# Pre-norm squares in column groups, a second block started inside the first, first weights in quarters: a two-block fp32 model on one core

## The chip, the core and the metric
The kernel runs on one core of one Trainium2 chip. The metric is device time in microseconds (us) of one execution; lower is better. Of the core's engines four compute: TensorE (PE, matmuls into PSUM), VectorE (DVE), ScalarE (ACT) and GpSimd (POOL). SyncE (SP) issues most DMAs. Every engine runs its own instructions in order, and they wait for each other by semaphores.

## What is computed
A residual stream h of 272 tokens (16 meta tokens and 256 of the input) by 1024 features goes through two blocks of a first model and one of a second. The parts, in the order of their weights' names:

```
for i in 0, 1:                       # the first model
    f = swiglu(rms_norm(h, g), w_gu, w_down);  h = h + 0.5 * rms_norm(f, g')     # gu0/dn0, gu2/dn2
    m = short_conv_mixer(...) if i == 0 else diff_attention_mixer(...)           # conv_in/out, qkv/attn_out
    h = h + rms_norm(m, g'')
    f = swiglu(rms_norm(h, ...), ...);         h = h + 0.5 * rms_norm(f, ...)    # gu1/dn1, gu3/dn3
h = h[:, 16:]                        # the second model
h = h + mixers(rmsnorm(h)) @ w_out                                               # mix_in, mix_out
h = h + square(relu(rmsnorm(h) @ w_ff1)) @ w_ff2                                 # ff1, ff2
out = rmsnorm(h)
```

All is float32. rms_norm(t, g) is t * rsqrt(mean(t * t) + eps) * g over the features. Nine of these norms are "pre-norms", of h itself: eight ahead of a matrix product and the final one.

## The kernel before
h lies with features on partitions, as eight tiles of 128 x 272 (k = 0 to 7). The weights, 225 MB, are streamed once as blocks of 16, 22 or 24 tiles of 128 x 128 into four buffers w_raw. To keep float32 accuracy at the speed of the fp32r type, each operand is split in a high part (rounded to fp32r) and a low part (the rest): w = w_hi + w_lo, x = x_hi + x_lo. A product is then three fp32r passes per tile, w_hi x_hi, w_hi x_lo and w_lo x_hi (lines 1370 to 1372). ACT makes w_hi (`split_hi`, line 446) and DVE makes w_lo (`split_lo`, line 813). There are two buffers of each, so the split of block n waits until TensorE has used block n - 2. Inside each engine's program the split of block i + 2 (`next_hi`, `next_lo`) is written between the elementwise work on block i; that place in the program sets when it can start.

A pre-norm is not applied to the input. x is h times the gain; the product is made with it, and the result is multiplied by rstd, which is known later. So at the entry of every part, `first_block` (line 1387) goes through k: two or three x_hi matmuls with w_hi and with w_lo, then those with x_lo, and then `add_square` (line 1381), a plain f32 matmul of `ones` with the square of h tile k, which adds up the sum over features in PSUM bank `SUM`. ACT makes x_hi and the square for each k (`pre_norm`), and its square k waits for the squares matmul of k - 2. After the eighth, `root` makes rstd: DVE takes ms from PSUM, ACT does Ln and Exp (lines 470, 472), DVE three Newton steps (829 to 834). DVE then multiplies the block's results by rstd (`take`, line 868), ACT applies silu, and so on.

Ahead of six of the eight entries stands a post-norm (`post_norm`, line 849): h is updated tile by tile by DVE (scaled, h, x_lo), while TensorE runs `keep_warm`, seven f32 matmuls of 384 columns on constants (line 1436). At the start, SP loads the first weight block whole, then the parameters, then h, then three more blocks.

The second block's split of each entry is made between the post-norm's root and the pre-norm (`second_hi`) and after the x_lo parts (`second_lo`).

## Times and profile before
| | us |
|---|---|
| median of 3 runs | 1453.66 |
| lowest, highest | 1453.46, 1454.67 |
| the profiled execution's own time | 1454.77 |
| its span, first to last instruction | 1453.0 |
| TensorE busy | 1402.9 (97%) |
| VectorE, ScalarE busy | 896.7 (62%), 653.5 (45%) |
| mean granted TensorE clock | 0.992 |

In the rows below, PE is TensorE's matmuls and PEld its weight loads. A row of a timeline gives the start, the time, the engine, the line of the kernel, the operation, out<-in, and in brackets how long the engine was idle before it and what ended that. An f32 matmul shows as two records (x2). The time of a matmul's record includes its way through the array; where matmuls follow each other, the distance of their starts is what one costs.

### The profile page before, as it was taken

The page shows a single profiled execution, that of the slowest core. Times are in us where ns is not written, and L with a number is a line of the kernel's source. Part 1 is how long each engine was busy: PE and PEld are TensorE (multiplying, and loading weights), DVE is VectorE, ACT ScalarE, POOL GpSimd, SP SyncE. Part 2 cuts the span into 40 slices and gives each one's busy share as a digit, 9 for nine tenths or more (in the row PEclk, how much of TensorE's full clock was granted, in tenths as well). Part 3 has the DMA queues.
Part 4 walks back from the last instruction along what each step waited for, and adds up shares of the span by engine and source line. Part 5 has one row for each costly group of instructions (what it writes and reads, how often), then busy time and mean ns, then how long its engine had stood idle before and what let it go on. Part 6 is the DMA issues. An engine that isn't in the chain of part 4 may idle for free.

```text
span 1453.0 us, 26632 instructions
## 1 busy us (share of the span) xinstructions
PE 1402.9 (97%) x10924; PEld 1361.8 (94%) x10924; DVE 896.7 (62%) x1329; ACT 653.5 (45%) x925; POOL 12.5 (1%) x26
## 2 busy tenths in 40 slices
PE   6999999999999999999999999999999997999997
PEld 6999999998999999999998988999998986899997
DVE  4666547657666537666457877666546566577543
ACT  5444435345444435444444555544535425444332
POOL 0000000000000000000000000000001100000000
PEclk9999999999999999999999999999999999999999
DMA  6555543343555433555553223455653411355550
GB/s 241 174 173 206 199 173 131 131 135 126 173 174 205 174 142 117 173 173 210 181 183 112 82 84 117 167 181 192 231 184 127 175 59 59 125 194 180 196 175 30
DMA packets 29353, 227.54 MB, mean 157 GB/s; under 512 B 3376, under 2 KB 4672, under 8 KB 5088
## 3 DMA queue, kind: packets, MB, share of 16 engines
q1 hardware_dynamic: 28656, 224.75, 44.0%
q0 software_dynamic: 624, 1.77, 0.3%
q8 instruction: 51, 0.84, 0.2%
q14 instruction: 22, 0.18, 0.0%
HBM read 225.44 MB, written 1.06 MB: 156 GB/s over the span
## 4 chain that ended last, share of the span: by engine, by line
PE 84%; DVE 10%; ACT 4%; issue 2%; DMA 0%; DVEq 0%; ACTq 0%
PE ps L1370 24%; PE ps L1372 24%; PE ps L1371 24%; DVE w_lo L813 4%; PE ps L1384 2%; ACT w_hi L446 2%; PE ps L1436 2%; PE ps L1395 1%; PE ps L1396 1%; PE ps L1400 1%; ACT s_exp L594 1%; DVE small L1009 0%; PE ps L1576 0%; PE ps L1578 0%; PE ps L1577 0%
## 5 line engine op out<-in xcount | busy, mean ns | idle before, releaser
L813 DVE TENSOR_TENSOR w_lo<-w_raw,w_hi 128x2048 fp32r<-128x2048 f32 (+2 forms) x188 | 482.0, 2564 | 232.7 <-ACT w_hi L446 232.7
L1370 PE MATMUL ps<-x_hi,w_hi 128*128 128x272 f32 (+1 forms) x2136 | 616.1, 288 | 5.9 <-DVE w_lo L813 5.7
L1372 PE MATMUL ps<-x_hi,w_lo 128*128 128x272 f32 (+1 forms) x2136 | 612.5, 287 | 0.0
L1371 PE MATMUL ps<-x_lo,w_hi 128*128 128x272 f32 (+1 forms) x2136 | 610.7, 286 | 0.0
L446 ACT ACTIVATE w_hi<-w_raw 128x2048 fp32r<-128x2048 f32 (+2 forms) x188 | 401.1, 2134 | 425.9 <-PE ps L1372 420.1
L1370 PEld LDWEIGHTS ps<-x_hi,w_hi 128*128 128x128 f32 x2136 | 403.8, 189 | 13.4 <-DVE w_lo L813 7.2
L1372 PEld LDWEIGHTS ps<-x_hi,w_lo 128*128 128x128 f32 x2136 | 403.9, 189 | 0.0
L1371 PEld LDWEIGHTS ps<-x_lo,w_hi 128*128 128x128 f32 x2136 | 403.5, 189 | 0.3 <-issue 0.2
L1370 PE MATMUL ps<-hid_hi,w_hi 128*128 128x272 f32 (+1 forms) x960 | 276.1, 288 | 0.2 <-DVE w_lo L813 0.2
L1372 PE MATMUL ps<-hid_hi,w_lo 128*128 128x272 f32 (+1 forms) x960 | 274.8, 286 | 0.0
L1371 PE MATMUL ps<-hid_lo,w_hi 128*128 128x272 f32 (+1 forms) x960 | 273.7, 285 | 0.0
L1370 PEld LDWEIGHTS ps<-hid_hi,w_hi 128*128 128x128 f32 x960 | 181.0, 189 | 0.8 <-issue 0.4
L1371 PEld LDWEIGHTS ps<-hid_lo,w_hi 128*128 128x128 f32 x960 | 181.0, 189 | 0.2
L1372 PEld LDWEIGHTS ps<-hid_hi,w_lo 128*128 128x128 f32 x960 | 181.0, 189 | 0.0
L872 DVE TENSOR_TENSOR gate<-rstd,ps 128x272 f32<-128x272 f32 (+1 forms) x88 | 38.2, 434 | 106.8 <-PE ps L1372 106.2
L504 ACT ACTIVATE square<-ps 128x272 f32<-128x272 f32 (+1 forms) x40 | 15.8, 395 | 152.7 <-PE ps L1372 150.7
L1395 PE MATMUL ps<-x_hi,w_hi 128*128 128x272 f32 (+1 forms) x152 | 54.1, 378 | 12.8 <-DVE w_lo L813 10.0
L905 DVE TENSOR_TENSOR sumsq<-sumsq,square 128x272 f32<-128x272 f32 (+1 forms) x42 | 18.3, 435 | 65.0 <-ACT square L504 64.8
L480 ACT ACTIVATE square<-h 128x272 f32<-128x272 f32 (+1 forms) x72 | 30.2, 420 | 34.7 <-PE ps L1384 24.0
L1384 PE MATMUL ps<-square,ones 128*128 128x272 f32 (+1 forms) x144 | 45.0, 395 | 0.6 <-ACT square L480 0.6
L1395 PEld LDWEIGHTS ps<-x_hi,w_hi 128*128 128x128 f32 x152 | 29.6, 195 | 16.3 <-issue 13.5
L842 DVE SCALAR_TENSOR_TENSOR x_lo<-h,par,x_hi 128x272 fp32r<-128x272 f32 (+1 forms) x64 | 31.3, 492 | 21.5 <-ACT x_hi L493 21.5
...
## 6 DMA issues: line engine op xcount, KB each, us to landing
w_raw<-w_gu SPq DMA_DIRECT2D x88, 1024.0 KB, 4.9
...
w_raw<-w_ff SPq DMA_DIRECT2D x32, 1024.0 KB, 4.9
...
w_raw<-w_conv_out SPq DMA_DIRECT2D x4, 1024.0 KB, 4.8
w_raw<-w_attn_out SPq DMA_DIRECT2D x4, 1024.0 KB, 5.0
```

The costliest lines, as they stand in the source:

```text
L446: act.activation(w_hi[j % SPLIT][:, 0:width], w_raw[j][:, 0:width], ACT.Copy).then_inc(hi_ready, 1)
L480: act.activation(square[k % 2][:, c0:T], h[:, k, c0:T], ACT.Square).then_inc(h_sq_ready, 1)
L813: dve.tensor_tensor(w_lo[j % SPLIT][:, 0:width], w_raw[j][:, 0:width], w_hi[j % SPLIT][:, 0:width].bitcast(F32), ALU.subtract).then_inc(lo ...
L842: dve.scalar_tensor_tensor(out=x_lo[:, k, c0:T], in0=h[:, k, c0:T], scalar=par[:, g:g + 1], in1=x_hi[:, k, c0:T].bitcast(F32), op0=ALU.mul ...
L872: dve.tensor_tensor(gate[j % 2][:, 0:width], rstd[:, c0:T], ps[:, 2 * (j % 2), c0:T], ALU.mult)\
L905: dve.tensor_tensor(sumsq[:, c0:T], sumsq[:, c0:T], square[par_][:, c0:T], ALU.add).then_inc(sumsq_ready, 1)
L1370: pe.matmul(out_ap, w_hi[slot][:, cols], hi(k), start=first, stop=False)
L1371: pe.matmul(out_ap, w_hi[slot][:, cols], lo(k), start=False, stop=False)
L1372: mm = pe.matmul(out_ap, w_lo[slot][:, cols], hi(k), start=False, stop=last)
L1384: pe.matmul(ps[:, SUM, c0:T], ones[:, :], square[k % 2][:, c0:T], start=k == 0, stop=k == KD - 1)\
L1395: pe.matmul(o, w_hi[0][:, cols], x_hi[:, k, c:T], start=k == 0, stop=False)
L1436: pe.matmul(ps[:, 5, 0:3 * P], ones[:, :], sq3[:, :], start=True, stop=True)
```

## The change
Nothing that is computed changes but the way in which the squares are added. The parts:
- **Squares in groups.** The squares of all eight tiles go to fx (free at that time) and no longer to two small buffers, so ACT doesn't wait for TensorE between them. `group_squares` multiplies them with 32 columns of ones each, tile k into the column group k mod 4 of the array, accumulated in PSUM; ACT copies the result, scaled by 1/32, to SBUF (`copy_groups`), and `sum_groups` adds the groups with one matmul of ones. Both stand later than the squares did: after the low passes of the second block and at its end in an ffn and ff1; between the three products of the second block in conv_in and mix_in; after the first block and in the second in qkv.
- **Ahead.** In gu1, gu2, gu3 and ff1, `first_block` also makes, for each k, the passes w_hi x_hi of the second block (two) and one of the two w_hi x_lo; `second_block` does the rest. The first block's results lie in banks 4 and 5.
- **Splits earlier.** ACT's split of the third block stands ahead of the root (ffn, conv_in, ff1), DVE's too in an ffn and in ff1, but not in conv_in.
- **post_norm** on DVE: h of tile k directly after scaled of tile k (x_lo of k - 2 between them).
- **First weights in pieces.** The first block comes in four DMAs, each a quarter of the columns of both halves (rows of 1 KB), h in four DMAs and the parameters, issued by ACT; the first splits go by quarters.
- **Warming** with 26 fp32r passes of 272 (256) columns.
- The mixers' low part has a tile of its own, and its g_q memset waits for that matmul.

```diff
-            def add_square(q, k, c0):
-                pe.wait_ge(h_sq_ready, KD * q + k + 1)
-                pe.matmul(ps[:, SUM, c0:T], ones[:, :], square[k % 2][:, c0:T], start=k == 0, stop=k == KD - 1)\
-                  .then_inc(h_sq_summed, 1)
+            def group_squares(q, c0, count=KD):
+                for k in range(count):
+                    g = GROUP * (k % GROUPS)
+                    pe.wait_ge(h_sq_ready, KD * q + k + 1)
+                    mm = pe.matmul(ps[g:g + GROUP, SUM + 1, c0:T], ones[:, 0:GROUP], fx[:, k, c0:T],
+                                   start=k < GROUPS, stop=k + GROUPS >= count, tile_position=(0, g))
+                mm.then_inc(h_sq_grouped, 1)
+            def sum_groups(q, c0):
+                pe.wait_ge(h_sq_copied, q + 1)
+                pe.matmul(ps[:, SUM, c0:T], ones[:, :], h_sum[:, c0:T], start=True, stop=q < 8).then_inc(h_sq_summed, 1)
...
-                    add_square(q, k, c0)
+                    for s, (o, c) in enumerate(ahead):
+                        cols = slice((s * KD + k) * P, (s * KD + k + 1) * P)
+                        pe.matmul(o, w_hi[1][:, cols], x_hi[:, k, c:T], start=k == 0, stop=False)
+                        if s == 0:
+                            pe.matmul(o, w_hi[1][:, cols], x_lo[:, k, c:T], start=False, stop=False)
+            def second_block(q, n0, outs, c0, ahead):
+                pe.wait_ge(hi_ready, n0 + 2)
...
+                        if not ahead or s == 1:
+                            pe.matmul(o, w_hi[1][:, cols], x_lo[:, k, c0:T], start=False, stop=False)
+                group_squares(q, c0)
+                split_ready(n0, 1)
...
+                        mm = pe.matmul(o, w_lo[1][:, cols], x_hi[:, k, c0:T], start=False, stop=k == KD - 1)
+                mm.then_inc(block_used, 1)
+                sum_groups(q, c0)
...
-                pe.wait_ge(consts_loaded, 16)
-                for _ in range(count):
-                    pe.matmul(ps[:, 5, 0:3 * P], ones[:, :], sq3[:, :], start=True, stop=True)
+                warm = y_hi[:, 0, :] if u == 1 else z_hi[:, 0, :] if u == 4 else hid_hi[:, first_col(u):T]
+                for _ in range(26):
+                    pe.matmul(ps[:, 5, 0:warm.shape[-1]], warm[:, 0:P], warm, start=True, stop=True)
...
                     for s in range(3):
                         mm = product(ps[:, b + s, 0:T], j % 2, s * KD, KD, hi, lo)
+                        if isinstance(i, int) and i == 1 and s < 2:
+                            (group_squares if s == 0 else sum_groups)(q, 0)
...
# ACT, pre_norm
-                if KD * q + k >= 2:
-                    act.wait_ge(h_sq_summed, KD * q + k - 1)
-                act.activation(square[k % 2][:, c0:T], h[:, k, c0:T], ACT.Square).then_inc(h_sq_ready, 1)
+                act.activation(fx[:, k, c0:T], h[:, k, c0:T], ACT.Square).then_inc(h_sq_ready, 1)
...
+                if name:
+                    next_hi(name, count, 0, 0)
+                copy_groups(q, c0)
                 root(s, c0)
...
+            act.dma_start(par[:, :], params).then_inc(par_loaded, 16)
+            for q in range(PIECES):
+                ks = slice(q * KD // PIECES, (q + 1) * KD // PIECES)
+                act.dma_start(h[:, ks, :], h_in[:, ks, :]).then_inc(h_landed[q], 16)
# DVE, root
+                if meanwhile:
+                    next_lo(*meanwhile, 0, 0)
                 dve.wait_ge(summed, count)
...
-                pre_root(u, s, c0)
+                pre_root(u, s, c0, *((f"gu{f}", GU_N) if kind == "ffn" else ()))
```

What stands in a row on the engines, at two places. First TensorE at the entry of gu1, from the last warming to the end of the first k step (w_hi, w_lo are the parts of the weights, the first block's except in lines 1473 and 1475, which are the second's), before:

```order
L1436 MATMUL ps<-sq,ones 128x384 x7
L1395 MATMUL ps<-x_hi,w_hi 128x272
L1396 MATMUL ps<-x_hi,w_lo 128x272
L1395 MATMUL ps<-x_hi,w_hi 128x272
L1396 MATMUL ps<-x_hi,w_lo 128x272
L1400 MATMUL ps<-x_lo,w_hi 128x272 x2
L1384 MATMUL ps<-square,ones 128x272
```

And after, with the end of the loop and the rest of the second block:

```order
L1463 MATMUL ps<-x_hi,w_hi 128x272
L1464 MATMUL ps<-x_hi,w_lo 128x272
L1468 MATMUL ps<-x_lo,w_hi 128x272 x2
L1473 MATMUL ps<-x_hi,w_hi 128x272
L1475 MATMUL ps<-x_lo,w_hi 128x272
L1473 MATMUL ps<-x_hi,w_hi 128x272
L1486 MATMUL ps<-x_lo,w_hi 128x272 x8
L1438 MATMUL ps<-fx,ones 32x272 x8
L1492 MATMUL ps<-x_hi,w_lo 128x272 x16
L1445 MATMUL ps<-h_sum,ones 128x272
```

The square left the step, three passes of the second block came in, and the eight squares and their sum stand in the second block. Second, VectorE at the entry of conv_in, from the split of the second block (line 813, later 853) to that of the third, before:

```order
L813 TENSOR_TENSOR w_lo<-w_raw,w_hi 128x3072
L827 TENSOR_SCALAR ms<-ps 128x272
L829 TENSOR_TENSOR rstd<-r 128x272
L831 SCALAR_TENSOR_TENSOR rstd<-rstd,ms 128x272
L834 SCALAR_TENSOR_TENSOR rstd<-rstd,r 128x272
L923 TENSOR_TENSOR rstd_sq<-rstd 128x272
L924 MEMSET cv_u 128x2
L932 TENSOR_TENSOR cv_c<-rstd_sq,ps 128x272
L933 TENSOR_TENSOR cv_b<-rstd,ps 128x272
L935 TENSOR_TENSOR cv_u<-cv_c,ps 128x272
L813 TENSOR_TENSOR w_lo<-w_raw,w_hi 128x3072
```

And after:

```order
L853 TENSOR_TENSOR w_lo<-w_raw,w_hi 128x3072
L875 TENSOR_SCALAR ms<-ps 128x272
L877 TENSOR_TENSOR rstd<-r 128x272
L879 SCALAR_TENSOR_TENSOR rstd<-rstd,ms 128x272
L882 SCALAR_TENSOR_TENSOR rstd<-rstd,r 128x272
L971 TENSOR_TENSOR rstd_sq<-rstd 128x272
L972 MEMSET cv_u 128x2
L980 TENSOR_TENSOR cv_c<-rstd_sq,ps 128x272
L981 TENSOR_TENSOR cv_b<-rstd,ps 128x272
L983 TENSOR_TENSOR cv_u<-cv_c,ps 128x272
L853 TENSOR_TENSOR w_lo<-w_raw,w_hi 128x3072
```

Here nothing moved on VectorE; what ms waits for did, on TensorE.

## Rows read from the trace of the kernel before

**Rows 1.** The page: busy time and share by engine; shares of the chain.
```profile
PE 1402.9 (97%) x10924; PEld 1361.8 (94%) x10924; DVE 896.7 (62%) x1329; ACT 653.5 (45%) x925; POOL 12.5 (1%) x26
...
PE 84%; DVE 10%; ACT 4%; issue 2%; DMA 0%; DVEq 0%; ACTq 0%
```

**Rows 2.** Chain of waits, entry of gu1: start, us, what.
```profile
333.06 4.52 PE ps L1436 x14
...
338.32 0.46 PE ps L1384 x2
```

**Rows 3.** Waits of PE: us in total, times, longest.
```profile
PE ps L1395 <- DVE w_lo L813: 10.0, 1, 10.0
PE ps L1370 <- DVE w_lo L813: 7.9, 9, 2.2
...
PE ps L1395 <- ACT x_hi L493: 2.8, 2, 2.5
```

**Rows 4.** Timeline of PE, gu1: start, us, work [idle before].
```profile
337.11 0.58 PE L1395 MATMUL ps<-x_hi,w_hi 128*128 128x272 f32 x1
...
354.37 0.39 PE L1370 MATMUL ps<-x_hi,w_hi 128*128 128x272 f32 x1 [0.69 <-DVE w_lo L813]
...
360.51 0.29 PE L1370 MATMUL ps<-x_hi,w_hi 128*128 128x272 f32 x1
```

**Rows 5.** Timeline of ACT and DVE, entry of gu1.
```profile
336.22 0.52 ACT L493 ACTIVATE x_hi<-h,par 128x272 fp32r<-128x272 f32 x1 [0.84 <-DVE h L860]
...
347.29 0.44 DVE L827 TENSOR_SCALAR ms<-ps 128x272 f32<-128x272 f32 x1
...
350.12 0.44 DVE L872 TENSOR_TENSOR gate<-rstd,ps 128x272 f32<-128x272 f32 x1
...
351.80 0.41 ACT L514 ACTIVATE gate<-gate 128x272 f32<-128x272 f32 x1
...
351.93 2.29 DVE L813 TENSOR_TENSOR w_lo<-w_raw,w_hi 128x2048 fp32r<-128x2048 f32 x1 [1.01 <-ACT w_hi L446]
```

**Rows 6.** Timeline of DVE, entry of conv_in.
```profile
234.90 3.35 DVE L813 TENSOR_TENSOR w_lo<-w_raw,w_hi 128x3072 fp32r<-128x3072 f32 x1
238.32 0.44 DVE L827 TENSOR_SCALAR ms<-ps 128x272 f32<-128x272 f32 x1
...
242.68 3.35 DVE L813 TENSOR_TENSOR w_lo<-w_raw,w_hi 128x3072 fp32r<-128x3072 f32 x1
```

**Rows 7.** Timeline of ACT and PE at the start.
```profile
5.62 1.91 ACT L446 ACTIVATE w_hi<-w_raw 128x2048 fp32r<-128x2048 f32 x1 [3.53 <-DMA w_raw<-w_gu]
...
9.96 0.56 PE L1395 MATMUL ps<-x_hi,w_hi 128*128 128x272 f32 x1 [9.96 <-DVE w_lo L813]
...
23.70 0.59 PE L1370 MATMUL ps<-x_hi,w_hi 128*128 128x272 f32 x1 [2.23 <-DVE w_lo L813]
```

**Rows 8.** Groups by line and form: count, busy us, mean ns, idle before.
```profile
L1283 DVE TENSOR_TENSOR hid<-hid 128x512 f32<-128x512 f32 x16 | 11.1, 692 | 0.5
...
L763 ACT ACTIVATE hid_hi<-hid 128x512 f32 x12 | 7.4, 616 | 2.1 <-DVE hid L1283 2.1
```

**Rows 9.** Timeline of PE, one scores step of the attention.
```profile
792.05 0.97 PE L1533 MATMUL ps<-k_rot,q_rot 64*128 64x144 f32 x8 [0.32 <-DVE k_rot L1001]
792.96 0.40 PE L1370 MATMUL ps<-x_hi,w_hi 128*128 128x272 f32 x1
```

**Rows 10.** Windows: us, busy by engine (x), PEclk (granted), DMA share, GB/s.
```profile
24.00:27.00 3.00, 3.00 (x14) 3.00 (x14) 1.95 (x5) 2.91 (x4) 0.00 (x0) 0.50 0.65 202
...
306.90:310.30 3.40, 1.47 (x12) 1.25 (x12) 2.58 (x2) 1.56 (x3) 0.00 (x0) 1.00 0.02 5
310.40:313.70 3.30, 3.30 (x17) 3.30 (x16) 1.64 (x3) 2.51 (x3) 0.00 (x0) 0.50 0.76 233
```

**Rows 11.** DMA issues: KB each, median us from issue to landing.
```profile
w_raw<-w_gu SPq DMA_DIRECT2D x88, 1024.0 KB, 4.9
...
h<-h_in SPq DMA_DIRECT2D x1, 1088.0 KB, 6.7
```

More of the change, by code:

```diff
@@ L62 @@
 RAW, SPLIT = 4, 2
+PIECES = 4
+GROUPS = 4
+GROUP = P // GROUPS
 SLOT = TRI_T * P
@@ L549, in step @@
                 def step(i, j, last=False):
-                    if not last:
+                    if not last and i > 0:
                         next_hi("conv_in", TRI_N, i, j)
@@ L760, in step @@
                 def step(i, j):
-                    next_hi("ff1", FF1_N, i, j)
+                    if not isinstance(i, int) or i > 0:
+                        next_hi("ff1", FF1_N, i, j)
                     act.wait_ge(hid_ready, i + (4 * KF + 1))
@@ L764, in step @@
                        .then_inc(hid_hi_ready, 1)
-                loop(act, FF1_N, step, peel=2)
+                step(0, 0)
+                loop(act, FF1_N, step, first=1, peel=2)
+            act.dma_start(par[:, :], params).then_inc(par_loaded, 16)
+            for q in range(PIECES):
+                ks = slice(q * KD // PIECES, (q + 1) * KD // PIECES)
+                act.dma_start(h[:, ks, :], h_in[:, ks, :]).then_inc(h_landed[q], 16)
             act.preload_act_table_set(LN_EXP_SET)
-            split_hi(0, 0, WIDTH[0])
             act.wait_ge(eps_ready, 2)
@@ L775, in _ @@
                 c0 = first_col(u)
-                pre_norm(u, s, c0, pre)
+                pre_norm(u, s, c0, pre, *{"ffn": (f"gu{f}", GU_N), "conv": ("conv_in", TRI_N), "attn": ()}[kind])
                 s += 1
@@ L1288, in step @@
                        .then_inc(hid_lo_ready, 1)
-                loop(dve, FF1_N, step, peel=2)
+                step(0, 0)
+                loop(dve, FF1_N, step, first=1, peel=2)
             def second_lo(q):
@@ L1402, in first_block @@
                         mm.then_inc(block_used, 1)
-                    add_square(q, k, c0)
+                    for s, (o, c) in enumerate(ahead):
[4 more added lines that the diff above has]
+            def second_block(q, n0, outs, c0, ahead):
+                pe.wait_ge(hi_ready, n0 + 2)
+                for s, o in enumerate(outs):
+                    for k in range(KD):
+                        cols = slice((s * KD + k) * P, (s * KD + k + 1) * P)
+                        if not ahead:
+                            pe.matmul(o, w_hi[1][:, cols], x_hi[:, k, c0:T], start=k == 0, stop=False)
+                        if not ahead or s == 1:
+                            pe.matmul(o, w_hi[1][:, cols], x_lo[:, k, c0:T], start=False, stop=False)
+                group_squares(q, c0)
+                split_ready(n0, 1)
+                for s, o in enumerate(outs):
+                    for k in range(KD):
+                        cols = slice((s * KD + k) * P, (s * KD + k + 1) * P)
+                        mm = pe.matmul(o, w_lo[1][:, cols], x_hi[:, k, c0:T], start=False, stop=k == KD - 1)
+                mm.then_inc(block_used, 1)
+                sum_groups(q, c0)
             def hidden(name, f, q, c0):
@@ L1452, in convolution @@
                 hi, lo = x_parts(0)
-                first_block(q, n0, [(ps[:, s, 0:T], 0) for s in range(3)], 0)
+                first_block(q, n0, [(ps[:, s, 0:T], 0) for s in range(3)])
                 def step(i, j):
@@ L1629, in mixers @@
                     if i == 0:
-                        first_block(q, n0, [(ps[:, s, 0:SEQ], META) for s in range(3)], META)
-                        pe.wait_ge(mix_loaded, 6 * 16)
-                        pe.wait_ge(mix_zeroed, 4)
-                        pe.matmul(ps[0:HEADS, 7, :], rel_sb[:, :], onehot_sb[:, :], start=True, stop=True)\
-                          .then_inc(dist_done, 1)
+                        first_block(q, n0, [(ps[:, s, 0:SEQ], META) for s in range(3)])
                         continue
@@ L1641, in mixers @@
                         mm = product(ps[:, 3 * (i % 2) + s, 0:SEQ], i % 2, s * KD, KD, hi, lo)
+                        if i == 1 and s < 2:
+                            (group_squares if s == 0 else sum_groups)(q, META)
                     mm.then_inc(block_used, 1)
                     if i == 1:
+                        pe.wait_ge(mix_loaded, 6 * 16)
+                        pe.wait_ge(mix_zeroed, 4)
+                        pe.matmul(ps[0:HEADS, 7, :], rel_sb[:, :], onehot_sb[:, :], start=True, stop=True)\
+                          .then_inc(dist_done, 1)
                         pe.wait_ge(low_ready, KD)
@@ L1647, in mixers @@
                         for k in range(KD):
-                            mm = pe.matmul(ps[0:16, 6, 0:SEQ], w_glow_sb[:, k, :], fx[:, k, META:T], start=k == 0, stop=k == KD - 1)
+                            mm = pe.matmul(ps[0:16, 6, 0:SEQ], w_glow_sb[:, k, :], low[:, k, :], start=k == 0, stop=k == KD - 1)
                         mm.then_inc(g_pe, 1)
@@ L1773, in wide_hidden @@
                 hi, lo = x_parts(META)
[L1775 removed]
+                ahead = ((ps[:, 2, 0:SEQ], META), (ps[:, 3, 0:SEQ], META))
+                first_block(q, n0, [(ps[:, AHEAD + s, 0:SEQ], META) for s in range(2)], ahead)
+                second_block(q, n0, [ps[:, 2, 0:SEQ], ps[:, 3, 0:SEQ]], META, ahead)
                 def step(i, j):
                     split_ready(n0, i)
[L1779 removed]
+                    if not isinstance(i, int) or i >= 3:
                         pe.wait_ge(relu_ready, i * 2 - 2)
```

132 lines of the change are left out of this document (87 added, 45 removed).

## The prediction
> **What bounds the kernel now.** I read the page's busy shares and its chain first: TensorE is busy for 97% of the span and holds 84% of the chain that ended last [rows 1]. An edit pays only by taking work off TensorE or by closing one of its waits. The waits are few: 10.0 us ahead of the first matmul, nine waits for a w_lo split that come to 7.9 us (the longest 2.2), and 2.5 us for x_hi ahead of ff1 [rows 3]. Then I read the places where a pre-norm stands, since the change touches little else. There a plain f32 squares matmul stands in the chain with 0.46 us, and seven warming matmuls with 4.52 us [rows 2]; an fp32r pass is far cheaper: 48 of them lie between 354.37 and 360.51, 0.126 us each and 6.05 us a block [rows 4].
>
> **Squares.** Eight at 0.455 us are 3.64 us at each of nine pre-norms. After the change the eight load 32 columns of weights each, for four column groups of the array, and one more f32 matmul (0.455) sums the groups. No row shows column groups. The nearest is the scores stage, where f32 matmuls of 64 rows alternate between the two halves of the array: two products of 144 and two of 272 columns would take 1.39 us one after another, and start at 792.05 with the next matmul at 792.96 [rows 9]: 0.91 us, half of 1.39 and 0.2 for filling and draining. So the halves run side by side. Bounds for the eight are 0.91 us (four side by side) and 3.64 us (none); I take the lower, by that row, and add the 0.2. With the sum it is 1.57 us: TensorE's work falls by 2.1 us a place, 1.95 with 256 columns.
> The Trainium skill, TensorEngine Tiling (Array Packing), Key Properties, says that a change of tiling mode drains the engine: the 0.2 agrees. Its page TensorE: Matmul & The Clock Gate, Measured speedup vs the span model, gives three column groups 2.38 times the speed, not 3; by that the eight would cost an estimated 0.24 us more, 2 us in all; no run here shows it.
>
> **Warming.** 26 fp32r passes take 3.3 us where 4.5 stood: -1.2 us at six places (-1.4 with 256 columns). What they don't cover comes back as a wait for x_hi, counted below.
>
> **What is late next: the root.** The squares' sum stood at the end of the first block; now it stands behind the second block (ffn, ff1) or behind two thirds of it (conv_in, mix_in). rstd moves with it, and behind rstd are queued, on ScalarE and VectorE, the splits of a later block. In an ffn the chain is 2.83 us from ms to gate (347.29 to 350.12), gate 0.44, silu 0.41 [rows 5], w_hi 1.92, w_lo 2.29, hand-overs 0.2: 8.1 us. TensorE has one block to hide it, 6.05 us: it waits 2.05 us ahead of the fourth block, where it had waited 0.69 ahead of the third [rows 4]. In conv_in VectorE's next w_lo starts 4.36 us after ms (238.32 to 242.68) and lasts 3.35 [rows 6]: 8.0 us behind the sum with hand-overs, against one product of 24 passes, 3.0 us: 4.9 us of wait that is not there now. ScalarE's w_hi comes early, but VectorE keeps w_lo behind the root.
>
> **Place by place** (warming, squares, waits after, waits before; minus is a gain).
> - gu1 and gu2: warming ends at 333.06 + 3.3 = 336.4; x_hi, now at 336.22 [rows 5], comes 0.24 earlier (h right behind its scaled), done at 336.5, TensorE starts 0.5 before 337.11. So -1.2 - 2.1 + (0.35 for x_hi + 0.5 for the first x_lo + 2.05) - (0.2 + 0.69) = -1.3 each. The second block's 24 high passes in the loop are moved, not removed: nine passes a k, 1.13 us, about VectorE's pace of three instructions (0.36 to 0.41 each beside one another). Its w_lo is ready before TensorE has done the squares, since the next w_lo stands behind it and ahead of the root: no wait there.
> - gu3: -1.4 - 1.95 + (1.5 + 0.5 + 2.2) - 1.7 = -0.8.
> - conv_in: the first block without squares ends at 224.5 + 0.5 + 72 x 0.126 = 234.1. VectorE, no longer held by the squares, starts w_lo at 232.7 instead of 234.90 [rows 6]; it is ready at 236.1, 2.0 later than TensorE. -1.2 - 2.1 + (0.4 + 2.0 + 4.9) - 0 = +4.0.
> - qkv: -3.3 + (0.6 for x_hi, 1.2 for w_lo, 2.1 for the query's copy, which ScalarE does behind the root, 2.9 for rotary) - 2.1 = +1.4.
> - mix_in: -3.35 + (0.7 + 2.05 + 0.5 + 2.6) = +2.5. The 2.6: eight copies into low, w_hi and a w_lo of 3.35 follow the later root. qkv and mix_in have more links than I can price: 2 us either way each.
> - ff1: -1.95; root 2.8, two relu, square 0.69, hid_hi 0.61 [rows 8], hid_lo 0.69, relu and square again, w_lo 2.29: 9.4 against 5.7, 3.65 waited where 1.0 was: +0.7.
> - Final norm: eight squares off the last products, a group of seven and two f32 matmuls on: -1.6.
> - gu0: TensorE starts at 9.96 behind w_hi (from 5.62) and w_lo, and waits till 23.70 for block two [rows 7]. With quarters ScalarE issues five DMAs (0.42 each, as SP's), loads its table (1.28), is free at 4.2, and does a quarter of w_hi, two x_hi, two squares in 2.05 us: four in 12.4, w_hi of block two at 14.3. TensorE then has 32 passes, squares, 16 passes, sum: 21.9; block three to 28.0, a wait of 2.1: block four starts at 30.1. Now it starts at 37.5 (23.70 + two blocks + 1.5 for the clock below + 0.2): -7.5. The bound on the other side: h took 6.7 us to land, a weight block 4.9 [rows 11], and now rows of 1 KB and two queues share the engines; if the last quarter lands 5 us late, -2.5. I take -7.5.
> Sum: -7.5 + 4.0 - 2.6 - 0.8 + 1.4 + 2.5 + 0.7 - 1.6 = -3.9 us.
>
> **The clock.** After the wait that ends at 23.70 the granted clock is 0.50, the lower level, from 24 to 27; a stretch with 1.47 us busy of 3.40 (1.93 idle) at 307 to 310 is followed by 0.50 too [rows 10]. No wait of 1.5 us in the list [rows 3] was followed by it. At 1.2 GHz a pass takes 0.226 us, so 3.4 us there lose 3.4 x (1 - 0.126 / 0.226) = 1.5. The change has eleven waits of 1.9 to 4.9 us that were shorter or absent. Bounds: none to ten stretches more, 0 to 15 us. Most waits are just above 1.93, so I take four: +6.0.
> Total +2.1. On the profiled execution's own 1454.77 (span 1453.0) it is 1456.9; the median of the runs stands 1.1 below that execution: 1456.
>
> **Rivals.**
> - *The other side, slower: column groups don't overlap.* Place: the eight squares matmuls at nine pre-norms. One at a time they take 3.64 instead of 0.91, 2.7 x 9 = +24.6: 1480. Two at a time +8: 1464. For it: no column group in the trace, and each carries a wait of its own. Against: the halves in the scores stage [rows 9]. From some 2 us for the eight the kernel is slower by more than 0.2%.
> - *Faster: the clock holds.* Seven of the eleven waits are 2.0 to 2.2 us. If none lowers the clock, the sum is -3.9: 1450.
> - *The quarters land late*, so the start is not what the change means it to be: +5: 1461.
>
> **Chances.** Forecast 0.5 (its own range 1450 to 1461, none to seven stretches); no overlap 0.1; two at a time 0.1; clock holds 0.2; late quarters 0.1. 0.2%, 2.9 us, is about what a measurement of this kernel can tell from no change: 1450.8 to 1456.6. Faster takes the clock's case and 0.05 of the forecast's: 0.25. Same takes 0.34 of the forecast's and its neighbours'. Slower the rest, 0.41. Range 1448 to 1472: out are the full loss of overlap and a gain beyond the clock's case.
>
> **What would show it.** The records of the eight squares within 1.3 us; the first matmul near 5.7 us; waits for w_lo of 2 us ahead of the fourth block of each ffn, 4.9 in conv_in, 3.6 in ff1; clock 0.50 behind about half of them. I am wrong if the eight take 2 us or more, if those waits are under 1 us, or if the first matmul starts after 8 us.

## The result, and the profile after

| | before | after |
|---|---|---|
| median of 17 runs, us | 1454.53 | 1462.63 |
| lowest, highest | 1452.64, 1457.69 | 1457.79, 1467.47 |
| mean granted clock over runs (before: 23 later runs) | 0.993 | 0.986 |
| profiled execution's span, us | 1453.0 | 1457.6 |

The ratio is 1.005, 95% interval 1.004 to 1.0061: slower, by 8.1 us of the medians. The forecast was 1456, inside a range that holds 1462.6, and slower was its likeliest sign (0.41); but the forecast's own range ended at 1461, and the median lies where it had put its rivals. The profiled execution (1459.38) is one of the faster ones; the two slowest, 1465.64 and 1467.47, have a granted clock of 0.984 and 0.983, the two fastest 0.989.

Busy time and the chain's shares, on the page of the changed kernel, beside [rows 1]:

```profile
PE 1385.4 (95%) x11014; PEld 1353.4 (93%) x11014; DVE 896.6 (62%) x1332; ACT 655.6 (45%) x937; POOL 12.6 (1%) x26
...
PE 79%; DVE 14%; ACT 5%; issue 2%; DMA 0%; DVEq 0%; ACTq 0%; SPq 0%
```

TensorE's work fell by 17.5 us, and the span rose by 4.6: the chain's share of TensorE went from 84 to 79%, that of VectorE from 10 to 14. The waits of TensorE say where (in all, times, longest), beside [rows 3]:

```profile
PE ps L1422 <- DVE w_lo L853: 25.9, 12, 4.8
PE ps L1463 <- DVE w_lo L867: 6.9, 1, 6.9
PE ps L1463 <- ACT x_hi L524: 6.4, 7, 2.6
PE ps L1629 <- DVE k_rot L1049: 5.7, 8, 1.5
...
PE ps L1422 <- ACT q_sb L605: 1.7, 1, 1.7
```

The one wait at the start fell from 10.0 to 6.9; the waits for w_lo inside rose from 7.9 to 25.9 us. The entry of gu1 on TensorE, beside [rows 4] (x16 are the eight squares, two records each):

```profile
336.80 0.36 PE L1463 MATMUL ps<-x_hi,w_hi 128*128 128x272 f32 x1 [0.36 <-ACT x_hi L524]
...
341.00 0.29 PE L1463 MATMUL ps<-x_hi,w_hi 128*128 128x272 f32 x1
...
347.45 1.12 PE L1438 MATMUL ps<-fx,ones 128*32 128x272 f32 x16
...
348.51 2.27 PE L1492 MATMUL ps<-x_hi,w_lo 128*128 128x272 f32 x16
...
359.29 0.38 PE L1422 MATMUL ps<-x_hi,w_hi 128*128 128x272 f32 x1 [2.01 <-DVE w_lo L853]
```

The eight squares take 1.05 us to the next matmul (1.00 with 256 columns); the loop goes by 1.13 us a k; the third block is reached without a wait, and the fourth waits 2.01. What it waits for, on VectorE, ScalarE and VectorE, beside [rows 5]:

```profile
351.27 0.44 DVE L875 TENSOR_SCALAR ms<-ps 128x272 f32<-128x272 f32 x1 [0.77 <-PE ps L1445]
...
354.10 0.44 DVE L921 TENSOR_TENSOR gate<-rstd,ps 128x272 f32<-128x272 f32 x1
...
354.91 1.90 ACT L466 ACTIVATE w_hi<-w_raw 128x2048 fp32r<-128x2048 f32 x1
...
356.85 2.29 DVE L853 TENSOR_TENSOR w_lo<-w_raw,w_hi 128x2048 fp32r<-128x2048 f32 x1 [0.91 <-ACT w_hi L466]
```

From ms at 351.27 to the end of w_lo at 359.14 it is 7.87 us, and TensorE has one block of 6.05. The entry of conv_in, beside [rows 6]:

```profile
230.15 0.39 PE L1422 MATMUL ps<-x_hi,w_hi 128*128 128x272 f32 x1 [1.76 <-DVE w_lo L853]
...
238.21 0.44 DVE L875 TENSOR_SCALAR ms<-ps 128x272 f32<-128x272 f32 x1 [8.12 <-PE ps L1445]
...
242.57 3.35 DVE L853 TENSOR_TENSOR w_lo<-w_raw,w_hi 128x3072 fp32r<-128x3072 f32 x1
...
245.98 0.55 PE L1422 MATMUL ps<-x_hi,w_hi 128*128 128x272 f32 x1 [4.79 <-DVE w_lo L853]
```

w_lo of the third block (242.57) again stands 4.36 us behind ms, and 4.79 are waited for it. The start, beside [rows 7]:

```profile
5.34 0.63 ACT L471 ACTIVATE w_hi<-w_raw 128x512 fp32r<-128x512 f32 x1 [0.49 <-DMA w_raw<-w_gu]
...
6.87 0.57 PE L1463 MATMUL ps<-x_hi,w_hi 128*128 128x272 f32 x1 [6.87 <-DVE w_lo L867]
...
15.45 0.39 PE L1484 MATMUL ps<-x_hi,w_hi 128*128 128x272 f32 x1 [0.68 <-ACT w_hi L466]
...
31.50 0.39 PE L1422 MATMUL ps<-x_hi,w_hi 128*128 128x272 f32 x1 [2.00 <-DVE w_lo L853]
```

The clock. Stretches of the changed kernel with the columns of [rows 10]; the second and third hold gu1's wait of 2.01, with no fall behind it:

```profile
246.30:249.30 3.00, 3.00 (x15) 3.00 (x15) 2.43 (x7) 1.92 (x2) 0.00 (x0) 0.50 0.72 218
354.90:359.30 4.40, 2.39 (x20) 2.17 (x19) 3.49 (x5) 4.39 (x5) 0.00 (x0) 1.00 0.02 9
359.40:362.40 3.00, 3.00 (x24) 3.00 (x25) 2.96 (x5) 0.86 (x2) 0.00 (x0) 1.00 0.63 205
570.60:573.60 3.00, 3.00 (x15) 3.00 (x15) 2.52 (x2) 0.43 (x1) 0.00 (x0) 0.50 0.80 320
775.30:778.30 3.00, 3.00 (x16) 3.00 (x16) 2.93 (x14) 2.47 (x1) 0.00 (x0) 0.50 0.01 3
904.80:907.80 3.00, 3.00 (x16) 3.00 (x16) 3.00 (x10) 2.25 (x6) 0.00 (x0) 0.51 0.00 0
1280.50:1283.50 3.00, 3.00 (x16) 3.00 (x15) 3.00 (x3) 0.64 (x1) 0.00 (x0) 0.50 0.80 317
```

Five stretches of 3.4 us at 0.50, 1.2 GHz, are new: behind the waits of 4.79 in conv_in, 2.01 in gu2 (569), 1.68 in qkv, two of 1.47 at gu3's entry, and 3.67 in ff1. The one of before at 24 is gone (granted 1.00 there). Both kernels also have one of 3.4 at 310 (after: 311), one of 6.8 at 1205 (1209), one of 3.4 at 1252 (1256) and the last 6.0 (6.7) us of the span, behind TensorE's last matmul.

| part | forecast, without new stretches | measured | of it new stretches |
|---|---|---|---|
| gu0 | -7.5 | -5.8 | 0 |
| conv_in | +4.0 | +5.9 | +1.5 |
| gu1 | -1.3 | -1.3 | 0 |
| gu2 | -1.3 | +0.3 | +1.5 |
| qkv | +1.4 | +1.6 | +1.5 |
| gu3 | -0.8 | +0.5 | +1.5 |
| mix_in | +2.5 | +2.7 | 0 |
| ff1 and the end | -0.9 | +0.8 | +1.5 |
| sum | -3.9 | +4.7 | +7.5 |

Measured is how the difference of the two profiled executions grows from one post-norm's sum of squares to the next (219.07 against 213.29, 330.95 against 331.08, and so on; ff1 by its first matmul and the last one of the program). Without the new stretches it is -2.8, beside the forecast's -3.9; both count the stretch at 24 that went, -1.5.

### The profile page after: what moved, and what is told of

It reads as the page before. It is cut to its first block, busy times and chain, and to the rows that moved or that the text cites. A ratio compares the mean times of both kernels' runs of the same rounds, so it can differ in the third digit from the quotient of the medians.

```text
span 1457.6 us, 26741 instructions
## 1 busy us (share of the span) xinstructions
PE 1385.4 (95%) x11014; PEld 1353.4 (93%) x11014; DVE 896.6 (62%) x1332; ACT 655.6 (45%) x937; POOL 12.6 (1%) x26
## 4 chain that ended last, share of the span: by engine, by line
PE 79%; DVE 14%; ACT 5%; issue 2%; DMA 0%; DVEq 0%; ACTq 0%; SPq 0%
PE ps L1422 24%; PE ps L1424 23%; PE ps L1423 23%; DVE w_lo L853 4%; ACT w_hi L466 2%; DVE scaled L904 1%; DVE h L910 1%; PE ps L1492 1%; DVE x_lo L890 1%; ACT s_exp L627 1%; PE ps L1468 1%; PE ps L1473 1%; PE ps L1438 1%; PE ps L1463 1%; PE ps L1464 1%
## 5 line engine op out<-in xcount | busy, mean ns | idle before, releaser
L1422 PE MATMUL ps<-x_hi,w_hi 128*128 128x272 f32 (+1 forms) x2056 | 595.7, 290 | 25.4 <-DVE w_lo L853 23.7
L1424 PE MATMUL ps<-x_hi,w_lo 128*128 128x272 f32 (+1 forms) x2056 | 590.7, 287 | 0.0
L1423 PE MATMUL ps<-x_lo,w_hi 128*128 128x272 f32 (+1 forms) x2056 | 589.6, 287 | 0.0
L1422 PEld LDWEIGHTS ps<-x_hi,w_hi 128*128 128x128 f32 x2056 | 390.4, 190 | 32.1 <-DVE w_lo L853 17.2
L1424 PEld LDWEIGHTS ps<-x_hi,w_lo 128*128 128x128 f32 x2056 | 390.7, 190 | 0.0
L1423 PEld LDWEIGHTS ps<-x_lo,w_hi 128*128 128x128 f32 x2056 | 389.9, 190 | 0.6 <-issue 0.2
L953 DVE TENSOR_TENSOR sumsq<-sumsq,square 128x272 f32<-128x272 f32 (+1 forms) x42 | 18.3, 435 | 65.0 <-ACT square L538 64.8
L1463 PE MATMUL ps<-x_hi,w_hi 128*128 128x272 f32 (+1 forms) x152 | 42.2, 300 | 13.2 <-DVE w_lo L867 6.9
L1463 PEld LDWEIGHTS ps<-x_hi,w_hi 128*128 128x128 f32 x152 | 30.3, 199 | 14.5 <-issue 14.5
L552 ACT ACTIVATE hid_hi<-up 128x272 f32 (+3 forms) x88 | 36.6, 416 | 14.3 <-DVE up L930 14.3
L1464 PE MATMUL ps<-x_hi,w_lo 128*128 128x272 f32 (+1 forms) x152 | 41.6, 295 | 0.0
L935 DVE TENSOR_TENSOR hid_lo<-up,hid_hi 128x272 f32 (+3 forms) x88 | 37.9, 431 | 2.0 <-ACT hid_hi L552 2.0
```

The lines of the kernel that those rows point to most:

```text
L552: act.activation(hid_hi[:, bass.ds(i * T + c0, width)], up[j % 2][:, 0:width], ACT.Copy)\
L935: dve.tensor_tensor(hid_lo[:, bass.ds(at, width)], up[j % 2][:, 0:width], hid_hi[:, bass.ds(at, width)].bitcast(F32), ALU.subtract).then_i ...
L953: dve.tensor_tensor(sumsq[:, c0:T], sumsq[:, c0:T], square[par_][:, c0:T], ALU.add).then_inc(sumsq_ready, 1)
L1422: pe.matmul(out_ap, w_hi[slot][:, cols], hi(k), start=first, stop=False)
L1423: pe.matmul(out_ap, w_hi[slot][:, cols], lo(k), start=False, stop=False)
L1424: mm = pe.matmul(out_ap, w_lo[slot][:, cols], hi(k), start=False, stop=last)
```

## The experiments

A term of all that follows: with a mean granted clock c and a span S, 2 x (1 - c) x S us were spent at 0.50, and 0.442 of them were lost (0.126 us a pass against 0.226). The last column takes that off; it is an estimate, good to a microsecond or so, since c has three digits. It also takes 0.442 of the 5 to 7 us at the end of every profiled span, where TensorE has nothing left and loses nothing, so only differences between rows mean something. "Without the clock" below is a difference of that column. The kernels ran in three sessions; the kernel before, in each of them, had a median of 1454.3 to 1454.5.

| kernel | runs | median, us | mean clock | us at 0.50 | mean span less the clock's loss |
|---|---|---|---|---|---|
| before | 23 | 1454.5 | 0.993 | 21 | 1443.7 |
| changed | 17 | 1462.6 | 0.986 | 42 | 1441.7 |
| e1_fill | 10 | 1455.5 | 0.992 | 24 | 1442.4 |
| e2_hi_first | 4 | 1438.2 | 0.989 | 31 | 1422.2 |
| e3_full_squares | 4 | 1479.8 | 0.986 | 41 | 1460.1 |
| e4_start_only | 7 | 1451.9 | 0.992 | 23 | 1439.9 |
| e5_best | 4 | 1428.2 | 0.995 | 15 | 1420.0 |
| e6_no_ahead | 4 | 1465.2 | 0.986 | 42 | 1445.7 |
| e8_early_sum | 5 | 1449.2 | 0.989 | 32 | 1434.6 |
| e9_both | 4 | 1427.9 | 0.994 | 16 | 1419.1 |
| e11_before_fixed | 4 | 1445.6 | 0.994 | 19 | 1435.7 |

**Warming in the new waits.**

```diff
+            def fill(bank, n, c0):
+                for _ in range(n):
+                    pe.matmul(ps[:, bank, c0:T], x_hi[:, 0, META:META + P], x_hi[:, 0, c0:T], start=True, stop=True)
...
                 step(2, 2)
+                fill(7, 14, c0)
                 loop(pe, GU_N, step, first=3)
```

> The changed kernel with fp32r warming passes put into its new waits and nothing moved: 14 ahead of the fourth block of each ffn, 13 and 36 ahead of the second and third block of conv_in, 12 in qkv, 15 and 18 in mix_in, 28 in ff1. They are cut to 0.1 to 0.3 us less than the waits in the trace of the changed kernel, and write banks that are free. Theory (the waits are long enough to lower the clock, and that costs more than the waits): of the five stretches at 0.50 that came in (246, 570, 774, 904, 1280 us) four go, the one at 904 stays (it follows waits for sumsq and x_hi, not filled); 1.5 us each is -6 against the profiled run, about -8 against the median of 1462.6: 1453 to 1456, granted clock 0.990 or more, and runs that lie within 4 us of each other. Rival (only the waits' own length counts): 1461 to 1464, clock 0.985 and the spread of 10 us as they were.

1455.5 (1451.8 to 1457.4), ratio to before 0.9999 (0.9986 to 1.0011): 7.1 us under the changed kernel, clock 0.992. The filled wait of conv_in on TensorE, and four windows behind filled waits:

```profile
241.01 4.61 PE L1449 MATMUL ps<-x_hi 128*128 128x272 f32 x36
```

```profile
243.00:246.00 3.00, 2.67 (x23) 2.46 (x21) 3.00 (x2) 0.18 (x1) 0.00 (x0) 1.00 0.00 0
246.00:249.00 3.00, 3.00 (x24) 3.00 (x25) 2.43 (x7) 1.65 (x2) 0.00 (x0) 1.00 0.66 184
568.00:571.00 3.00, 3.00 (x26) 3.00 (x25) 3.00 (x4) 0.86 (x2) 0.00 (x0) 1.00 0.71 251
1276.00:1280.00 4.00, 3.70 (x31) 3.49 (x31) 3.97 (x6) 1.87 (x2) 0.00 (x0) 1.00 0.48 145
```

No window at 0.50 where there had been three. The kernel without the clock's loss is the same as the changed one (1442.4 and 1441.7): within the estimate's microsecond nothing but the clock moved. The theory holds. In qkv the stretch only moved: TensorE no longer goes at the lower clock there, comes earlier to the scores and waits 2.72 for k_rot instead of 1.20, and the clock falls behind that. So not all was won: three of the four stretches went, and the spread was 5.6 us, not 4.

**TensorE's order in the waiting blocks.**

```diff
+            def hi_first(n0, i, outs, c0, sem_):
+                pe.wait_ge(hi_ready, i + (n0 + 1))
+                for s, o in enumerate(outs):
+                    for k in range(KD):
+                        cols = slice((s * KD + k) * P, (s * KD + k + 1) * P)
+                        pe.matmul(o, w_hi[i % 2][:, cols], x_hi[:, k, c0:T], start=k == 0, stop=False)
+                        pe.matmul(o, w_hi[i % 2][:, cols], x_lo[:, k, c0:T], start=False, stop=False)
+                    if sem_ and s < 2:
+                        sem_[s]()
+                split_ready(n0, i)
+                for s, o in enumerate(outs):
+                    for k in range(KD):
+                        cols = slice((s * KD + k) * P, (s * KD + k + 1) * P)
+                        mm = pe.matmul(o, w_lo[i % 2][:, cols], x_hi[:, k, c0:T], start=False, stop=k == KD - 1)
+                mm.then_inc(block_used, 1)
...
                 step(2, 2)
+                pe.wait_ge(gu_scaled, 3 * 2 + (2 * KF * f + 2))
+                hi_first(n0, 3, [ps[:, 2, c0:T], ps[:, 3, c0:T]], c0, None)
-                loop(pe, GU_N, step, first=3)
+                loop(pe, GU_N, step, first=4)
```

> The changed kernel, TensorE's order alone changed: in the blocks that wait for w_lo (fourth of each ffn and of ff1, second and third of conv_in and mix_in) all passes with w_hi stand ahead of those with w_lo, so that the wait for w_lo comes 4 to 6 us later. ScalarE and VectorE are as they were. Theory (TensorE waits there only because each tile asks for w_lo at once, and nothing else is late): of 25.9 us waited for w_lo all but some 5 go (ff1 still waits for w_hi, about 1.3, and for the relus of the second block, about 1), and with them four stretches at 0.50: 1462.6 - 20 - 8 = 1435, 1430 to 1440. Rival (the chain behind the root is the bound, and the wait comes back a block later, for w_lo of the fifth block or for a bank that VectorE has not read): the time falls by the clock alone, 1452 to 1457.

1438.2 (1435.6 to 1438.6), ratio 0.9878 (0.9858 to 0.9898), inside the theory's range. The waits of TensorE in this kernel, and its fourth block of conv_in:

```profile
PE ps L1648 <- DVE k_rot L1049: 6.7, 6, 2.7
...
PE ps L1422 <- DVE w_lo L853: 5.5, 5, 1.9
...
PE ps L1452 <- ACT w_hi L466: 1.2, 1, 1.2
```

```profile
247.34 0.39 PE L1422 MATMUL ps<-x_hi,w_hi 128*128 128x272 f32 x1 [1.69 <-DVE w_lo L853]
```

Of 25.9 us waited for w_lo 5.5 are left, 1.2 came for w_hi in ff1. In gu0 to gu3 and in mix_in the wait did not come back a block later; in conv_in 1.69 of it did, and in ff1 0.81: the chain behind the root is long, but it is not the bound. In the ffns and ff1 this is TensorE's order alone. In conv_in and mix_in it is not, whatever the expectation says: the squares and their sum stand behind the first two tiles (`sem_`), whose high passes are 16 and no longer 24 each, so ms came 15.1 us after conv_in's first matmul, where it was 19.2 (mix_in 14.2 and 18.3). There the order and an earlier root work together. The clock (0.989) gained less than the waits: ff1's 2.55 for x_hi and qkv's 2.71 for k_rot were still there, and a stretch at 0.50 followed each; a new one, of 6.8 us, came behind a wait of 1.44 for k_rot at 853.

**Squares 128 columns wide.**

```diff
-                    mm = pe.matmul(ps[g:g + GROUP, SUM + 1, c0:T], ones[:, 0:GROUP], fx[:, k, c0:T],
-                                   start=k < GROUPS, stop=k + GROUPS >= count, tile_position=(0, g))
+                    mm = pe.matmul(ps[:, SUM + 1, c0:T], ones[:, :], fx[:, k, c0:T],
+                                   start=k == 0, stop=k + 1 == count)
```

> The changed kernel with the eight squares matmuls in the same place but 128 columns of ones wide, not four groups of 32. In the trace of the changed kernel the eight take 1.05 us from the first to the next matmul (347.45 to 348.51), 1.00 with 256 columns. Theory (the column groups run side by side, which is where TensorE's work fell): 8 x 0.455 - 1.05 = 2.6 us more at each of eight places, 1.9 for the seven at the end, +22.7; where the sum's copy or w_lo was late anyway part of it is hidden (none in an ffn, whose root is on the path): +18 to +25, 1481 to 1487. Rival (the narrow weights or the place, not the groups, made them fast): +0 to +8, below 1471.

1479.8 (1479.1 to 1481.9), 17.1 us over the changed kernel. The eight and the next matmul in gu1:

```profile
354.05 3.83 PE L1437 MATMUL ps<-fx,ones 128*128 128x272 f32 x16
...
357.51 2.37 PE L1491 MATMUL ps<-x_hi,w_lo 128*128 128x272 f32 x16
```

3.46 us instead of 1.05. The distance to the next start leaves out part of the last matmul: to the start of the second pass behind them, less one pass of 0.126, it is 3.66 and 1.16 (3.46 and 1.11 with 256 columns). The two records of a wide one start 0.229 apart, 0.458 a matmul, the price of the single ones of before. Five places of 2.5, three of 2.35 and 1.9 at the end make 21.5; 0.9 of it lies in waits for w_lo that fall from 25.9 to 25.0 us. Without the clock the difference is 18.4, so 2 us of that sum don't show, and I can't say where; by the medians it is 17.1: a little under the range (1481 to 1487), and far from the rival's 8. e3 widens the weights and takes the groups away at once, so by itself it rules out the place, not the narrow weights. A row of the changed kernel settles that: in mix_in eight f32 matmuls of 16 columns stand in one group, with 256 columns moving:

```profile
1125.55 3.63 PE L1751 MATMUL ps<-low,w_glow_sb 128*16 128x256 f32 x16 [0.84 <-ACT low L704]
```

Their records start 0.216 us apart, 0.432 a matmul, and so do those of 128 columns in e3. Narrow weights alone gain nothing; the groups do run side by side.

**The start alone, in the kernel before.**

```diff
-                    load(0, 0)
-                    sp.dma_start(par[:, :], params).then_inc(par_loaded, 16)
-                    sp.dma_start(h[:, :, :], h_in).then_inc(h_loaded, 16)
+                    for q in range(PIECES):
+                        sp.dma_start(piece(w_raw[0], q), piece(w[name][0, :, :], q)).then_inc(piece_landed[q], 16)
...
-            split_hi(0, 0, WIDTH[0])
+                        if k % (KD // PIECES) == 0:
+                            first_hi(k // (KD // PIECES))
```

> The kernel before with the new start alone: first block in four DMAs, h in four and the parameters from ScalarE, first splits in quarters. Squares, blocks, warming as before. Theory (the start is the one large gain of the change, and it stands by itself): the first matmul at 6.9 us instead of 9.96, the first block ends near 17, where ScalarE's w_hi and VectorE's w_lo of the second block come as in the changed kernel, and the wait of 2.23 with its stretch at 0.50 goes: -4.5 to -7.5, 1447 to 1450. Rival (the start only helps because the squares left it: with them ScalarE and VectorE wait for TensorE's squares matmuls as before): -3 at most, 1451.5 or more.

1451.9 (1449.4 to 1454.4), ratio 0.997 (0.9955 to 0.9986): -2.6, and -3.8 without the clock. My theory missed, and the time is the rival's. The rival's reason shows on ScalarE and on TensorE:

```profile
9.78 0.43 ACT L494 ACTIVATE square<-h 128x272 f32<-128x272 f32 x1 [1.15 <-PE ps L1410]
...
12.04 0.43 ACT L494 ACTIVATE square<-h 128x272 f32<-128x272 f32 x1 [1.42 <-PE ps L1410]
...
17.62 1.90 ACT L454 ACTIVATE w_hi<-w_raw 128x2048 fp32r<-128x2048 f32 x1
...
21.90 0.39 PE L1396 MATMUL ps<-x_hi,w_hi 128*128 128x272 f32 x1 [2.24 <-DVE w_lo L832]
```

With two buffers for the squares ScalarE waits 1.15 and 1.42 us for TensorE's squares, comes to w_hi of the second block at 17.62 (13.49 in the changed kernel), and the wait of 2.24 at the second block stays as it was, with its stretch at 0.50. Of the 2.8 us by which the first matmul is earlier (7.13 for 9.96), 1.8 are left at the second block (21.90 for 23.70), and 1.8 at each of the six post-norms; why the runs' mean fell by 3.8 without the clock is open. In the changed kernel ScalarE is not held up, and with the squares gone the second block starts at 15.45.

**Without the passes ahead.**

```diff
-                ahead = ((ps[:, 2, c0:T], c0), (ps[:, 3, c0:T], c0)) if q > 0 else ()
+                ahead = ()
```

> The changed kernel without the second block's passes in the first block's loop (gu1, gu2, gu3, ff1); they stand behind it, ahead of the squares. Theory (the loop is paced by VectorE, and these passes are its filler): VectorE issues scaled, x_lo, h of one k each 1.12 us (338.31 to 339.43 in the trace of the changed kernel), TensorE needs 1.13 with the nine passes and 0.76 with six: the first block takes 7 x 1.12 + 0.76 = 8.6, the second 6.05, 14.9 with the start against 12.6 now, +2.3 in gu1, gu2 and gu3, about +1 in ff1, whose loop ScalarE paces: +8, 1467 to 1473. Rival (moving passes changes nothing): 1460 to 1464.

1465.2 (1463.8 to 1469.3), ratio 1.008 (1.0056 to 1.0103): +2.5, between the two, and +4.0 without the clock, half of what was worked out. TensorE in gu1's loop, and its squares:

```profile
341.22 0.29 PE L1463 MATMUL ps<-x_hi,w_hi 128*128 128x272 f32 x1
...
342.34 0.29 PE L1463 MATMUL ps<-x_hi,w_hi 128*128 128x272 f32 x1
...
351.32 1.12 PE L1438 MATMUL ps<-fx,ones 128*32 128x272 f32 x16
```

The k steps stay 1.12 apart with three passes less: VectorE paces them, as the theory says. From the first matmul to the fourth block it is 24.36 us against 22.49 in gu1, +1.9, and as much in gu2. But gu3 lost only 0.3, since a stretch at 0.50 lies in its loop in both kernels, in which TensorE and not VectorE is late, and ff1 nothing (24.03 and 24.02): ScalarE issues x_hi and square there each 0.70 us, about TensorE's 0.71 for six passes, so there was no gap to fill.

**The sum one product earlier in conv_in and mix_in.**

```diff
                 first_block(q, n0, [(ps[:, s, 0:T], 0) for s in range(3)])
+                group_squares(q, 0)
...
-                        if isinstance(i, int) and i == 1 and s < 2:
-                            (group_squares if s == 0 else sum_groups)(q, 0)
+                        if isinstance(i, int) and i == 1 and s == 0:
+                            sum_groups(q, 0)
```

> The changed kernel with the squares one product earlier in conv_in and mix_in: the groups right behind the first block, their sum behind the first of the second block's three products instead of the second. Theory (the splits wait because they are queued behind a root that starts late): the root starts 24 passes, 3.0 us (2.9 with 256 columns), earlier, and the wait for w_lo ahead of conv_in's third block falls from 4.79 to 1.8, that of mix_in's third from 2.42 to nothing, low's 0.84 too; the stretch at 0.50 at 246 goes: -3.0 - 3.2 - 1.5, 1453 to 1457. Rival (w_lo is late for another reason, ScalarE's w_hi or VectorE's own pace): no change beyond 2 us, 1460 or more.

1449.2 (1447.8 to 1453.9), ratio 0.9967 (0.995 to 0.9985): 13.5 us under the changed kernel, below the theory's range, and below the kernel before. TensorE ahead of conv_in's second and third block:

```profile
232.56 0.39 PE L1422 MATMUL ps<-x_hi,w_hi 128*128 128x272 f32 x1 [0.72 <-DVE w_lo L853]
...
244.10 0.39 PE L1422 MATMUL ps<-x_hi,w_hi 128*128 128x272 f32 x1 [1.75 <-DVE w_lo L853]
```

The wait ahead of the third block is 1.75, as worked out (4.79 - 3.0), and the squares, 1.05 us, now lie in the wait for the second block's w_lo, which falls from 1.76 to 0.72. That hiding I had left out, there and in mix_in (second block 0.94 for 1.92; the third still waits 0.59, where nothing was expected); without the clock the gain is 7.1 us where 6.2 was expected. The clock gave another 4.6 in the mean, 32 us at 0.50 for 42, where 1.5 was expected; the medians, 13.5 apart, lie 1.8 further apart than the means.

**All repairs on TensorE together.** e5_best is e2_hi_first with `hi_first` in the fourth block of conv_in and the second of conv_out and mix_out too, and:

```diff
+                        fill(5, 12, x_hi[:, 0, :])
                         part(i, 1)
+                        fill(5, 18, x_hi[:, 0, :])
                         turn_value(i - 1)
...
-                for _ in range(26):
+                for _ in range(36 if u == 4 else 26):
...
+                for _ in range(5):
+                    pe.matmul(ps[:, 7, 0:SEQ], ones[:, :], sq3[:, 0:SEQ], start=True, stop=True)
                 first_block(q, n0, [(ps[:, AHEAD + s, 0:SEQ], META) for s in range(2)], ahead)
```

> The kernel of e2_hi_first with what its trace still shows dealt with on TensorE alone: w_hi passes first in the fourth block of conv_in (it waits 1.69 for w_lo) and in the second of conv_out and mix_out (1.94); warming of 12 and 18 passes in qkv ahead of the query's part and of the scores (waits of 1.67 and 2.71), 36 instead of 26 passes ahead of gu3 (x_hi 1.47), five f32 matmuls of 256 columns ahead of ff1 (x_hi 2.55). Theory (a wait for w_lo can be passed by order, one for the root's chain only be filled): 3.6 us of waits go, and the stretches at 0.50 at 764 and 1235, 1.5 each: 1438.2 - 3.6 - 3.0 = 1431.6, 1429 to 1434. Rival (VectorE's splits are what paces those blocks, and the wait comes back behind them; the added warming is in the way of the waiting work): 1436 or more.

1428.2 (1426.8 to 1430.1), ratio 0.9819 (0.98 to 0.9838), 26 us under the kernel before and 0.8 below the range. The waits gave less than expected, 2.2 us of 3.6 without the clock, and the clock more, 7 for 3.0 (15 us at 0.50 for 31).

```profile
PE ps L1659 <- DVE k_rot L1049: 4.9, 8, 1.5
...
PE ps L1422 <- DVE w_lo L853: 3.6, 5, 1.1
PE ps L1484 <- ACT x_hi L524: 3.0, 7, 0.6
```

The rival was right in one place: of conv_out's 1.94 passed in the second block, 1.13 came back in a later one (305.64). And a wait alone did not decide the clock. The last scores step of qkv waits the same for k_rot in the kernel before (1.46, at 868.78) and here (1.45, at 851.17); behind it, first there, then here:

```profile
868.80:872.20 3.40, 3.40 (x29) 3.04 (x30) 2.68 (x5) 1.01 (x5) 0.00 (x0) 1.00 0.00 0
```

```profile
851.40:854.80 3.40, 3.40 (x18) 2.69 (x17) 2.09 (x5) 0.62 (x3) 0.00 (x0) 0.50 0.00 0
```

**And with the earlier sum.**

> The kernel of e5_best with the earlier squares and sum of e8_early_sum in conv_in and mix_in. Theory (both edits take away the same waits, for w_lo in conv_in and mix_in, and these are gone already): no change beyond noise, 1427 to 1430. Rival (the root that starts 3 us earlier also brings forward what follows it in those parts, as e8 fell by more than its two waits): another 2 to 4 us, 1424 to 1426.

1427.9 (1427.6 to 1429.2), ratio 0.9809 (0.9792 to 0.9825): the same, as the theory says. Both edits take away the same waits; and e5_best, like e2, has an earlier root in conv_in and mix_in already.

**The repairs without the change.** The kernel before, with `hi_first` in gu0's second block and the third of the ffns and ff1, and the five matmuls ahead of ff1.

> The kernel before with the repairs of e5_best where it has such waits, and nothing of the change: w_hi passes first in gu0's second block (it waits 2.23 for w_lo), in the third blocks of the ffns and ff1 (0.69, 0.70, 0.94, 0.61) and in the second of conv_out and mix_out (1.93), and five f32 matmuls ahead of ff1 (x_hi 2.55). Theory (the change saves TensorE's work, and its late roots only hid that): the old kernel gains these 7.1 us and the stretches at 0.50 at 24, 310 and 1252, 4.5 us: 1454.5 - 11.6 = 1443, 1441 to 1445, and e5_best at 1428 stays some 15 us ahead. Rival (the repairs are the whole gain and the change adds nothing to them): within 3 us of e5_best, 1431 or less.

1445.6 (1445.3 to 1446.6), ratio 0.9933 (0.9917 to 0.995): -8.9. TensorE still waits for w_hi in gu0 and for w_lo in conv_out:

```profile
28.52 0.36 PE L1393 MATMUL ps<-x_hi,w_hi 128*128 128x272 f32 x1 [0.58 <-ACT w_hi L446]
...
312.54 0.40 PE L1370 MATMUL ps<-y_hi,w_hi 128*128 128x272 f32 x1 [1.14 <-DVE w_lo L813]
```

That is 1.7 of the 7.1 us. The trace has lost the three stretches, as worked out, but has a new one of 3.4 us at 1195, 1.5 us: 11.6 - 1.7 - 1.5 is 8.4, near the 8.9 measured and 0.6 past the range. Over all runs the clock gave only 1 us (19 us at 0.50 for 21). e5_best is 17 us ahead of it (15.7 without the clock): the change is worth that, once its waits are passed.

Three parts of the change were not run by themselves: ScalarE's and VectorE's earlier split of the third block, the order in post_norm, and the warming in fp32r. Their prices in the forecast (warming -1.2 to -1.4 a place) are checked only within the sum of each place.

## Why the prediction came out as it did

**Squares: right.** The lower bound was taken from the scores stage [rows 9]: 0.91 and 0.2; it is 1.05, and without the groups the kernel is 17 us slower (e3), while narrow weights in one group take 0.432 each, as wide ones do. Both rivals, no overlap and two at a time, fall. The measured 3.46 for 1.05, or 3.66 for 1.16 with the last matmul whole, is a factor of 3.2 to 3.3 with four groups, fill and drain within it. The Trainium skill, TensorE: Matmul & The Clock Gate, Measured speedup vs the span model, whose 2.38 for three groups I had carried over to 0.24 us more for the eight, agrees in that the gain is less than the number of groups.

**The late root: right, place by place.** Forecast 2.05 us ahead of the fourth block, measured 2.00, 2.01, 2.01, 2.30; 1.9 to 2.0 and 4.9 in conv_in, measured 1.76 and 4.79; 3.65 in ff1, measured 3.67; 2.05 and 2.6 in mix_in, measured 1.92 and 2.42. That the root's place is the cause is shown by e8, in which 3.0 us earlier took 3.04 off the wait; that late splits, and nothing behind them, cost the time, by the ffns and ff1 in e2, where the splits stay as late and 12.0 us of waits for w_lo became 0.8, and 1.2 for w_hi. qkv was off, +0.1 for +1.4 without the clock: -3.3 as forecast, then 0.5, 0.82, 1.68 and 1.20 us of waits where I had 0.6, 1.2, 2.1 and 2.9, less the 0.85 of before, for which I had put 2.1. The 1.20 is at the lower clock; at the higher one it is the 2.7 of e1 and e2.

**The start: right in kind, 1.7 us too good.** The first matmul came at 6.87, not 5.7: ScalarE was free near 4.85, not 4.2, and the first quarter landed at 5.34 (the first row of the start above). The second block then waited 0.68 for w_hi, which I had not put, and the fourth began at 31.50 instead of 30.1. The +5 of the late quarters did not come: from 5.34 on ScalarE's splits follow its squares without a pause over 0.2 us.

**The clock: the step that was sized too low.** I put four new stretches, +6.0, and one less at the start, -1.5, which stood in the start's term: +4.5 for the clock and -2.4 for everything else. The profiled execution has five new ones and that one less. But one execution is one draw: over all runs the mean time at 0.50 rose from 21 to 42 us, six stretches, +9.2. Where the other executions have theirs no trace shows. Everything else came to -2.0 (mean spans without the clock's loss, 1443.7 and 1441.7), partly by luck: the start's miss of 1.7 one way and qkv's 1.3 the other cancel. So of the 6.6 us between forecast and median 0.4 are the work and the waits and 4.7 the clock; the rest, within a few tenths, is that the median of before is 1454.5 over 17 runs and was 1453.7 over the first three, and that the medians lie 8.1 apart and the means 7.3. e1 shows that this term alone decides the sign: with the waits filled and nothing else done, 8.1 us slower became 1.0, which is within its interval.

What I missed in it: a stretch came behind two waits of 1.47, ahead of gu3, 5.3 us apart. Neither was among the eleven that I had counted; I had gone by no wait of 1.5 us in [rows 3] being followed by 0.50, which holds for the kernel before but not for e2 and e5, where one of 1.45 was. I also passed over the 6.8 us at 0.50 from 1205, where waits of 0.6 to 1.3 us follow each other. And a wait of 2.0 is followed by a stretch in some places and not in others (359 no, 569 yes, in the same execution), so that a count can only be given as a mean.
